# Expert outputs summed on chip instead of through a DRAM tensor, with another layout of the chunks

## The chip, the cores and the metric

The kernel runs on one core of one Trainium2 chip. The metric is the device time of one execution in microseconds (us); the kernel before has a median of 1822.23 us in 3 runs (1821.59 to 1824.75).

## The reference, cut to what matters

Two layers stand one behind the other: a hybrid layer (state-space part and attention), and a block of depth 2 whose second feed-forward part is a mixture of experts. Everything is float32. Only the mixture is touched by the change: 256 tokens, 8 experts, each token goes to its two best experts, and the two results are summed with softmax weights. Then follow a gated embedding term and a layer norm.

```python
logits = (xf @ w_router).astype(jnp.float32)
top_vals, top_idx = lax.top_k(logits, TOP_K)          # TOP_K = 2 of 8
gates = jax.nn.softmax(top_vals, axis=-1)
...
    def block_fn(args):
        tok, e = args
        xb = xf[tok]
        return (jax.nn.silu(xb @ w1[e]) * (xb @ w3[e])) @ w2[e]   # w1, w3: 1024 x 3584, w2: 3584 x 1024
...
y = y * gate_buf[:, None].astype(y.dtype)
out = jax.ops.segment_sum(y, tok_buf, num_segments=n)
...
e = jax.nn.sigmoid(h @ ple_gate_w[i] + ple_gate_b[i]) * (p[i] @ ple_w[i])
h = layer_norm(DEEPNORM_ALPHA * h + f + e, ln2_g[i], ln2_b[i])
```

## The kernel before

Weights come as chunks of 128 x 2048 float32 (1 MB). The dense layers take 135 of them (`N_DENSE`); each expert has 42 (`E_CHUNKS`): seven steps (`E_STEPS`) of four chunks for w1 and w3 (c = 0 to 3) and two for w2 (c = 4, 5). In the mixture stage the chunks lie in nine places (`LATE_RING`); the SP queue issues the load into a place once TensorE has used the chunk that lay there (`chunks_used`).

The router ranks the experts by how many tokens they got. Ranks 1, 2 (the two middle experts) and 0 (the fullest) are "heavy": 128 rows each, and rank 0 has 64 rows more. A heavy chunk is split in two rounded parts: ScalarE rounds it (line 2361), VectorE takes the rest (line 3273), three chunks ahead (`LOOK`), and TensorE makes three products of each block, 12 matmuls in all. Ranks 4, 3, 5, 6 are "small": 32 rows, or 64 for rank 3, straight float32, with the output divided into four or two tiles. What overflows, and the last rank, goes through a loop of lists of 64 rows (`MAX_TRIPS` at most, one trip with these inputs), whose loads and products follow the 294 static chunks.

The static order is laid out by `_merged_order` before anything runs: after each heavy chunk a counter rises by `HEAVY_LOAD` - `PACE` (30 - 24; for the fullest expert `BIG_LOAD` 49), and small chunks, each of which lowers it (by 24 - 20 or 24 - 12), are put in until it is at or below zero. `AT[kind, step, c]` is a chunk's number in the order. Work between the chunks is hung on these numbers: `GATHER_AT` (TensorE gathers the rows of a list with a 0/1 matrix from VectorE, line 1617, into banks 6 and 7), `PLACES_AT` (transposes for the last list's weights), `HEAVY_TURN_AT` and `TURN_AT` (transposes of the hidden tiles, lines 1725 and 1638), and `EMBED_AT` (six embedding operations of the pool engine, lines 736 to 744).

Each list's output goes from its PSUM banks into an SBUF tile (`ysb`, `y_big`, `y_small`, `y_64`), and the pool engine's queue stores it in the DRAM tensor `y_rows` (lines 785 to 797). `ysb` and `y_small` are used again, so the copy of a later list waits for the store of an earlier one. At the end of each loop trip four indirect DMAs gather, for both token tiles and both choices, the 1024-wide rows from `y_rows` (line 811), and VectorE adds them to `fe` with weights (line 3311). Only the last list's 64 rows are combined on chip: TensorE multiplies `selT` with `y_small` (line 1796), and `last_norm` adds banks 0 to 3 to `fe` and norms it.

In the loop, a trip starts when VectorE has chosen the rows (`x_sel`); then TensorE gathers them (16 matmuls), ScalarE copies them to `loop_x`, and the 42 chunks follow in `LOOP_ORDER`.

Of the kernel before, what the change touches and what calls it, by code (L numbers as in the profile page):

```python
# [25 lines left out]
P = 128  # L26
# [33 lines left out]
Y_ROWS = EXTRA_ROW + (MAX_TRIPS - 1) * HALF  # L60
ZEROED = 16 * ((Y_ROWS - SPARE_ROW) // P)
# [32 lines left out]
C_ALL = C_PAIR + 2 * H_ATT  # L94
# [74 lines left out]
GATHERS = ((ROW_QUARTERS, P), (0, P), (ROW_64, P), (2 * P, P))  # L169
GATHER_AT = (AHEAD - 1, 12, 20, AT["heavy", E_STEPS - 1, 1])  # L170
# [5 lines left out]
def _hi_slots():  # L176

    used, slots = [-1, -2, -3, -3], {}
    for m in HEAVY:
# [3 lines left out]
        else:  # L183
# [6 lines left out]
Y_DONE = sorted([(AT["heavy", E_STEPS * e + E_STEPS - 1, 5], "heavy", e) for e in range(3)]  # L190
                + [(AT["small", E_STEPS * l + E_STEPS - 1, 5], "small", l) for l in range(N_SMALL)])
Y_PARTS = [TILED[n] if kind == "small" else 3 if n == 2 else 1 for _, kind, n in Y_DONE]
Y_STORES = sum(Y_PARTS)


def stored_by(kind, n):

    k = [part[1:] for part in Y_DONE].index((kind, n))
    return ZEROED + 16 * sum(Y_PARTS[:k + 1])


# [64 lines left out]
def build(nc, x, meta, consts, vecs, srow, rows, bv, tbias, pT, w_dense, w_moe, out):  # L266
    with ExitStack() as ctx:
        y_rows = nc.dram_tensor("y_rows", (Y_ROWS, D), F32).ap()

# [131 lines left out]
        xgT, xgR = rounded("xgT", 4096, KT, P), rounded("xgR", 26624, KT, P)  # L401
# [56 lines left out]
        def many(ap, n, axis=-1):  # L458
# [13 lines left out]
        ld_x, ld_meta, ld_cst, ld_vec, ld_small, x_in, moe_dma = (sem(n) for n in (  # L472
            "ld_x", "ld_meta", "ld_cst", "ld_vec", "ld_small", "x_in", "moe_dma"))
# [18 lines left out]
            "sums_in squares w_hi w_lo places m_g m_xga m_xgv m_ya m_yv m_cb m_fe y_kept x_sel x_run"  # L492
# [152 lines left out]
        def _(pool):  # L645
# [135 lines left out]
            def keep_tiled(first, y, n):  # L781

                for c in range(n):
                    cs, rs_ = slice(D // n * c, D // n * (c + 1)), slice(P // n * c, P // n * (c + 1))
                    pool.dma_start(y_rows[bass.ds(first, P // n), cs], y[rs_, 0:D // n]).then_inc(moe_dma, 16)

            for _, kind, n in Y_DONE:
                if kind == "small":
                    wait(pool, "s_y", n + 1)
                    keep_tiled(FIRST_ROW[n], y_small, TILED[n])  # L790
                elif n < 2:
                    wait(pool, "m_ya", n + 1)
                    wait(pool, "m_yv", n + 1)
                    pool.dma_start(y_rows[(n + 1) * P:(n + 2) * P, :], ysb).then_inc(moe_dma, 16)
                else:
                    wait(pool, "b_y", 2)
                    pool.dma_start(y_rows[0:P, :], y_big).then_inc(moe_dma, 16)
# [21 lines left out]
        def _(pe):  # L819
# [848 lines left out]
            def heavy_first(m, u, c):  # L1668

                d = u - MID_STEPS  # L1670
                if c == 0:
# [7 lines left out]
                    elif d > 0:  # L1679
                        wait(pe, "b_hT64", d)  # L1680
# [1789 lines left out]
```

## Time and profile before

| | |
|---|---|
| median of 3 runs | 1822.23 us |
| the profiled execution | 1822.1 us, its span 1820.3 us |
| TensorE (PE) busy | 1723.2 us, 95% |
| VectorE (DVE), ScalarE (ACT) | 986.4 us, 54%; 774.7 us, 43% |
| moved by DMA | 522.14 MB, 287 GB/s over the span |
| HBM read, written | 511.20 MB, 5.37 MB |
| chain that ended last | PE 70%, DMA 17%, DVE 6%, ACT 4% |

Times in the profile are microseconds from the span's start. PE is TensorE, PEld its weight loads, POOL the pool engine, SP the engine whose queue issues the weights. A busy share of matmuls is not the array's peak. DMA queue q1 is that of the weights, q0 the pool engine's (software) queue, q8 fetches instructions. The mixture stage is what happens after 940 us.

### The profile page before, as it was taken

The numbers are of one execution on the slowest core, as the hardware profiler recorded it, in microseconds if no ns is written. First come the engines' busy times: TensorE is split into PE (matmuls) and PEld (weight loads), VectorE is DVE, ScalarE is ACT, GpSimd is POOL, SyncE is SP. The second block draws the span as 40 slices with busy tenths as digits, with TensorE's granted clock in tenths as the row PEclk, the third lists the DMA queues.
The fourth block names the chain that finished last, engine by engine and source line by source line (L and its number), as shares of the span: only waits on it lengthen the run. The fifth ranks groups of instructions, "written<-read, shape, count | busy, mean of one in ns | idle before, by whom it ended". The sixth has DMA issues, their size and how long they took to land.

```text
span 1820.3 us, 30869 instructions
## 1 busy us (share of the span) xinstructions
PE 1723.2 (95%) x13024; PEld 1335.3 (73%) x13024; DVE 986.4 (54%) x1173; ACT 774.7 (43%) x995; POOL 148.6 (8%) x130
## 2 busy tenths in 40 slices
PE   9999999999999999999999999998989989998876
PEld 8977888777888899989878777776645656665532
DVE  6867643467767655577676676775222333332103
ACT  7766533345346433344735465653222232332001
POOL 0033000000102410000200000112000000000100
PEclk9999999999999999999999999999999999999899
DMA  6532474423672655558249999999999999999996
GB/s 255 197 116 93 162 251 177 166 90 122 242 236 91 239 185 185 185 180 279 78 160 407 411 421 416 419 421 421 420 421 420 421 420 420 420 419 414 411 421 258
DMA packets 78282, 522.14 MB, mean 287 GB/s; under 512 B 9264, under 2 KB 12592, under 8 KB 17600
## 3 DMA queue, kind: packets, MB, share of 16 engines
q1 hardware_dynamic: 72128, 499.50, 69.4%
q0 software_dynamic: 5408, 19.60, 3.0%
q8 instruction: 103, 1.69, 0.4%
q10 hardware_dynamic: 608, 1.07, 0.2%
q14 instruction: 35, 0.29, 0.0%
HBM read 511.20 MB, written 5.37 MB: 284 GB/s over the span
## 4 chain that ended last, share of the span: by engine, by line
PE 70%; DMA 17%; DVE 6%; ACT 4%; issue 3%; POOL 0%; DVEq 0%; ACTq 0%; SPq 0%
PE bank L836 62%; DMA arena<-in_w_moe 8%; DMA ring<-in_w_moe 8%; ACT whi L2361 2%; PE bank L1617 1%; PE bank L1051 1%; DVE wrest L2418 1%; DVE whi L3273 1%; PE bank L1415 1%; DVE wrest L3273 1%; DMA cst<-in_consts 1%; PE bank L1725 0%; PE bank L1054 0%; PE bank L1139 0%; PE bank L1638 0%
## 5 line engine op out<-in xcount | busy, mean ns | idle before, releaser
L2361 ACT ACTIVATE whi<-ring 128x2048 fp32r<-128x2048 f32 x82 | 156.6, 1914 | 176.9 <-DMA ring<-in_w_moe 176.9
L836 PE MATMUL bank<-ring,arena 128*32 128x128 f32 (+2 forms) x2600 | 181.4, 324 | 12.6 <-DMA ring<-in_w_moe 11.4
L3273 DVE TENSOR_TENSOR wrest<-ring,whi 128x2048 fp32r<-128x2048 f32 x54 | 127.4, 2361 | 81.5 <-ACT whi L2361 81.5
L836 PEld LDWEIGHTS bank<-ring,arena 128*32 128x32 f32 (+1 forms) x2600 | 110.9, 121 | 82.3 <-issue 41.1
L836 PE MATMUL bank<-hTh,wrest 128*128 128x256 f32 x608 | 169.7, 279 | 0.0
L3273 DVE TENSOR_TENSOR whi<-ring,whi 128x2048 fp32r<-128x2048 f32 x28 | 64.2, 2293 | 126.4 <-ACT whi L2361 126.4
L2418 DVE TENSOR_TENSOR wrest<-ring,fhi 128x2048 fp32r<-128x2048 f32 x33 | 76.9, 2331 | 80.9 <-ACT fhi L1831 80.8
L836 PEld LDWEIGHTS bank<-hTh,wrest 128*128 128x128 f32 x608 | 115.4, 190 | 0.0
L836 PE MATMUL bank<-whi,xgT 128*128 128x512 f32 x280 | 105.7, 410 | 3.1 <-issue 2.1
L836 PE MATMUL bank<-hTh,fhi 128*128 128x256 f32 x352 | 99.1, 281 | 0.0
L836 PE MATMUL bank<-hTr,fhi 128*128 128x256 f32 x352 | 98.8, 281 | 0.0
L1831 ACT ACTIVATE fhi<-ring 128x2048 fp32r<-128x2048 f32 x33 | 63.1, 1915 | 77.5 <-PE bank L836 77.5
L836 PE MATMUL bank<-whi,big_x 128*128 128x512 f32 x336 | 86.8, 408 | 9.7 <-DVE whi L3273 9.7
L836 PE MATMUL bank<-whi,hidE 128*128 128x512 f32 x232 | 86.5, 418 | 7.8 <-DVE hidR L3222 6.1
L836 PE MATMUL bank<-uTh,wrest 128*128 128x272 f32 (+1 forms) x320 | 89.4, 287 | 0.0
L836 PE MATMUL bank<-whi,xgR 128*128 128x512 f32 x224 | 88.8, 396 | 0.0
L836 PEld LDWEIGHTS bank<-whi,big_x 128*128 128x128 f32 x336 | 61.9, 191 | 31.4 <-DVE whi L3273 9.4
L2418 DVE TENSOR_TENSOR wrest<-ring,lhi 128x2048 fp32r<-128x2048 f32 x20 | 45.9, 2293 | 71.3 <-ACT lhi L1839 71.3
L836 PE MATMUL bank<-wrest,uTh 128*128 128x512 f32 (+1 forms) x208 | 82.0, 394 | 0.0
L836 PE MATMUL bank<-arena 128*32 128x128 f32 (+3 forms) x1168 | 80.8, 306 | 1.2 <-DMA arena<-in_w_moe 1.0
L3273 DVE TENSOR_TENSOR whi<-arena,whi 128x2048 fp32r<-128x2048 f32 x23 | 54.6, 2372 | 47.0 <-ACT whi L2361 46.8
L1839 ACT ACTIVATE lhi<-ring 128x2048 fp32r<-128x2048 f32 x20 | 38.3, 1916 | 78.3 <-PE bank L836 78.3
(569 smaller groups left out, 4146.3 us busy)
## 6 DMA issues: line engine op xcount, KB each, us to landing
ring<-in_w_moe SPq DMA_DIRECT2D x224, 1024.0 KB, 13.0
ring<-in_w_dense SPq DMA_DIRECT2D x135, 1024.0 KB, 4.8
arena<-in_w_moe SPq DMA_DIRECT2D x75, 1024.0 KB, 13.1
row<-in_w_moe SPq DMA_DIRECT2D x37, 1024.0 KB
row<-in_rows POOLq DMA_DIRECT2D x17, 512.0 KB, 5.6
arena<-arena SPq DMA_DIRECT2D x32, 106.5 KB, 4.1
arena<-in_tbias POOLq DMA_DIRECT2D x2, 1536.0 KB, 8.9
y_rows<-ncR POOLq DMA_DIRECT2D x3, 512.0 KB, 13.5
```

What stands on the lines that cost most here:

```text
L836: ins = pe.matmul(out_, lhsT, rhs, start=start, stop=stop, **more)
L1051: ins = pe.matmul(ps[5][:, r * HD:(r + 1) * HD], dec[:, j, r * P:(r + 1) * P], xdt[:, j, r * HD:(r + 1) * HD], start=True, stop=True, skip ...
L1415: S["s_ps"].on(pe.matmul(score_bank(u), q2[:, hh, j * P:(j + 1) * P], k2[:, hh // 2, :], start=True, stop=True))
L1617: ins = pe.matmul(ps[bank][:, at_:at_ + width], h[:, j, k * P:(k + 1) * P], sel[:, j, 0:width], start=j == 0, stop=j == 1, skip_group_chec ...
L1831: S["w_hi"].on(a.activation(hi, ring[:, c % RING, :], ACT.Copy))
L1839: S["w_hi"].on(a.activation(l1_hi(c), ring[:, c % RING, :], ACT.Copy))
L2361: S["w_hi"].on(a.activation(late_hi(b), late_raw(b), ACT.Copy))
L2418: S["w_lo"].on(v.tensor_tensor(wrest[:, s, :], ring[:, s, :], hi.bitcast(F32), ALU.subtract))
L3273: S["w_lo"].on(v.tensor_tensor(late_rest(b), late_raw(b), late_hi(b).bitcast(F32), ALU.subtract))
```

## The change

`y_rows`, its stores, its zero filling and the indirect gathers go. Each list's output is added to `fe` by way of TensorE: a picking matrix `selT` (rows of the list x 256 tokens, with the token's weight where it chose that row) times the output tile gives 128 tokens x 512 columns in a bank, which VectorE adds to `fe`.

- At chunk 36 TensorE spreads each token's row number and weight over all partitions (8 matmuls with a broadcast operand instead of two transposes), and VectorE keeps them as `all_dest`, `all_gate`. A picking matrix is then three VectorE operations of 128 x 256 (`pick`), with the row numbers in `row_id` (three new columns of the constants).
- The middle experts are summed in four rounds (`MID_ROUNDS`, chunks 90, 94, 134, 138 of the new order), each of two matmuls over 128 rows into two banks, then two additions.
- The fullest expert, its 64 rows and three small lists are summed in banks 0 to 3 by five `join`s at chunks 272, 275, 278, 281, 284 (`JOIN_AT`), behind the fullest expert's end, the fourth small list by a sixth after the last static chunk; four additions take the banks to `fe`. Lists of 32 rows are multiplied in two groups with a wait between them (`quarter_pieces`).
- The small lists have tiles of their own (`y_lists`), the second middle expert its own pair of gathered rows (`mid_x`), rounded right behind its gather instead of after the first expert's last use of the pair.
- The loop's first list is gathered at chunk 288, the next trip's at (4, 3) of each trip; the list before the loop's current one is summed at (2, 3).
- `PACE` is 24.8 instead of 24, so the whole order changes, and `EMBED_AT` moves from 78 to 117 to 46 to 85.

```diff
-EMBED_AT = (78, 86, 94, 102, 110, 117)
+EMBED_AT = (46, 54, 62, 70, 78, 85)
 LISTED_AT, CHOSEN_AT, PLACES_AT = 24, 30, 36
-FIRST_LOAD, HEAVY_LOAD, BIG_LOAD, SMALL_LOAD, PACE = 36, 30, 49, {2: 20, 4: 12}, 24
+FIRST_LOAD, HEAVY_LOAD, BIG_LOAD, SMALL_LOAD, PACE = 36, 30, 49, {2: 20, 4: 12}, 24.8
...
+BIG_DONE = _last("heavy", 2)
+MID_ROUNDS = (EMBED_AT[-1] + 5, EMBED_AT[-1] + 9, _last("heavy", 1) + 4, _last("heavy", 1) + 8)
+JOIN_AT = tuple(BIG_DONE + 3 + 3 * n for n in range(5))
+PICK_AT = (EMBED_AT[-1] + 4, _last("heavy", 1) - 2) + tuple(m - 2 for m in JOIN_AT) + (JOIN_AT[-1] + 2,)
+N_SUMS = len(MID_ROUNDS) + len(JOIN_AT) + 1
+N_ADDS = len(MID_ROUNDS) + 1
+GATHERS = ((ROW_QUARTERS, P), (0, P), (ROW_64, P), (2 * P, P), (EXTRA_ROW, HALF))
+GATHER_AT = (AHEAD - 1, 12, 20, AT["heavy", E_STEPS - 1, 1], JOIN_AT[-1] + 4)
...
+        mid_x = ((rounded("xgT", 4096, KT, P), rounded("xgR", 26624, KT, P)),
+                 (rounded("next_xgT", 2048, KT, P), rounded("next_xgR", 3072, KT, P)))
...
-            with pool.Fori(0, trips) as t:
-                wait(pool, "s_y", t + (N_SMALL + 1))
-                keep_tiled(t * HALF + SPARE_ROW, y_small, 2)
-                pool.wait_ge(moe_dma, t * 32 + (ZEROED + 16 * (Y_STORES + 2)))
-                S["y_kept"].on(pool.nop())
-                for n in range(4):
-                    pool.indirect_dma_start(yg[n], None, y_rows, bass.IndirectOffsetOnAxis(from_i[:, n:n + 1], 0)) \
-                        .then_inc(tb_in, 16)
-                pool.wait_ge(tb_in, t * 64 + (32 + 64))
...
+            def quarter_pieces(picks, y, stop):
+
+                for n in range(2):
+                    for q in range(4):
+                        t, c = divmod(q, 2)
+                        rows_ = half_columns(2 * c + n, QUARTER)
+                        ins = pe.matmul(ps[q][:, half_columns(n, SEQ)], picks[rows_, t * P:(t + 1) * P], y[rows_, :],
+                                        start=False, stop=stop, skip_group_check=True)
+                    if n == 0:
+                        S["c_half"].on(ins)
+                        pe.wait_ge(S["c_half"].sem, S["c_half"].n)
+                return ins
+
+            def mid_round(k):
+
+                e, t = divmod(k, 2)
+                wait(pe, "c_sel", e + 1)
+                wait(pe, "m_ya", e + 1)
+                wait(pe, "m_yv", e + 1)
+                wait(pe, "c_add", k if t else 0)
+                for c in range(2):
+                    ins = pieces(ps[(6, 2)[e] + c], 1, selT[e], ysb, t, c, True, True)
...
+            def join(k):
+
+                wait(pe, "c_sel", k + 3)
+                picks = selT[k % 2]
+                if k == 0:
+                    wait(pe, "b_y", 2)
+                    for q in range(4):
+                        ins = pieces(ps[q], 1, picks, y_big, q // 2, q % 2, True, False)
+                else:
+                    pe.wait_ge(S["c_ps"].sem, S["c_ps"].n)
+                    if k == 1:
+                        wait(pe, "b_whole", 1)
+                    else:
+                        wait(pe, "s_y", k - 1)
+                    if k in (1, 3):
+                        for q in range(4):
+                            ins = pieces(ps[q], 2, picks, y_64 if k == 1 else y_lists[1], q // 2, q % 2, False, False)
+                    else:
+                        ins = quarter_pieces(picks, y_lists[k - 2], k == 5)
+                S["c_ps"].on(ins)
...
+                    if (j, c) == (2, 3):
+                        wait(pe, "c_sel", t + (len(PICK_AT) + 1))
+                        wait(pe, "c_add", t + N_ADDS)
+                        for q in range(4):
+                            ins = pieces(ps[q], 2, selT[0], y_small, q // 2, q % 2, True, True)
+                        S["c_ps"].on(ins)
+                    elif (j, c) == (4, 3):
+                        wait(pe, "x_sel", t + (len(GATHERS) + 1))
+                        gather_list(HALF)
...
+            def pick(n, id_at, step):
+
+                step(v.scalar_tensor_tensor(second_T, all_dest[1], row_id[:, id_at:id_at + 1], all_gate[1],
+                                            ALU.is_equal, ALU.mult))
+                step(v.scalar_tensor_tensor(selT[n], all_dest[0], row_id[:, id_at:id_at + 1], all_gate[0],
+                                            ALU.is_equal, ALU.mult))
+                return v.tensor_tensor(selT[n], selT[n], second_T, ALU.add)
+
+            def pick_static(number):
+
+                if number:
+                    v.wait_ge(S["c_sel"].sem, number)
+                else:
+                    wait(v, "ple_done", 20)
+                    wait(v, "places", 3)
+                if number > 3:
+                    wait(v, "c_ps", number + 1)
+                S["c_sel"].on(pick(number % 2, number, fin))
...
+            def add_rows(bank, t, c):
+
+                cs = slice(512 * c, 512 * c + 512)
+                return v.tensor_tensor(fe[:, t, cs], fe[:, t, cs], bank[:, :], ALU.add)
+
+            def add_round(k):
+
+                e, t = divmod(k, 2)
+                wait(v, "c_ps", k + 1)
+                wait(v, "c_add", k)
+                for c in range(2):
+                    ins = add_rows(ps[(6, 2)[e] + c], t, c)
+                S["c_add"].on(ins)
```

## Rows read from the trace of the kernel before

**Rows 1.** The page's GB/s, in 40 slices of 45.5 us.

```profile
GB/s 255 197 116 93 162 251 177 166 90 122 242 236 91 239 185 185 185 180 279 78 160 407 411 421 416 419 421 421 420 421 420 421 420 420 420 419 414 411 421 258
```

**Rows 2.** Windows: busy us of PE, PEld, DVE, ACT, POOL; clock, DMA share, GB/s.

```profile
1000.00:1180.00 180.00, 173.57 (x1370) 131.61 (x1371) 127.13 (x109) 99.75 (x77) 8.13 (x2) 0.99 1.01 417
1600.00:1700.00 100.00, 87.45 (x1023) 58.92 (x1022) 30.52 (x29) 24.56 (x27) 2.58 (x5) 0.97 1.01 413
1740.00:1780.00 40.00, 30.55 (x218) 15.03 (x218) 0.84 (x2) 1.54 (x4) 0.00 (x0) 1.00 1.01 420
```

**Rows 3.** TensorE's products of whi and xgT: count, ns, first and last start.

```profile
L836 PE MATMUL bank<-whi,xgT x280: 387/395/628, 957.1 to 1296.5; 128*128 128x512 f32 x140
```

**Rows 4.** Timeline at the end: start, us, what.

```profile
1804.44 1.94 PE L836 MATMUL bank<-arena,bvr 128*64 128x512 f32 x8 [0.45 <-DMA arena<-in_w_moe]
...
1807.25 1.99 PE L1796 MATMUL bank<-arena 64*128 64x512 f32 x8 [0.87 <-ACT arena L2374]
```

**Rows 5.** DMA queues, 900 to 1820 us: packets, MB, share.

```profile
q0 software_dynamic: 1680, 4.85, 1.3%
q8 instruction: 57, 0.93, 0.4%
```

**Rows 6.** DMA queues, 1700 to 1806 us.

```profile
q0 software_dynamic: 800, 2.49, 5.9%
```

**Rows 7.** Timeline, last static chunk to the loop's first product.

```profile
1691.98 0.43 DVE L3256 COPY arena<-bank 128x256 f32<-128x256 f32 x1 [3.25 <-PE bank L836]
...
1694.29 6.58 PE L1617 MATMUL bank<-arena,h 128*128 128x64 f32 x32 [2.38 <-DVE arena L3298]
...
1701.64 5.37 PE L836 MATMUL bank<-ring,arena 128*64 128x256 f32 x32 [0.77 <-ACT arena L2366]
```

**Rows 8.** Timeline of TensorE in the static list.

```profile
1198.34 1.08 PE L836 MATMUL bank<-ring,arena 128*32 128x128 f32 x32
1199.35 0.50 PE L836 MATMUL bank<-whi,hidE 128*128 128x512 f32 x1
...
1205.13 1.08 PE L836 MATMUL bank<-ring,arena 128*32 128x128 f32 x32
...
1234.90 1.95 PE L836 MATMUL bank<-arena 128*64 128x256 f32 x16
1236.68 1.90 PE L836 MATMUL bank<-ring,arena 128*64 128x256 f32 x16
...
1601.83 1.95 PE L836 MATMUL bank<-arena 128*64 128x256 f32 x16
1603.70 0.33 PE L1638 MATMUL bank<-cst,arena 128*128 128x128 f32 x1
```

**Rows 9.** Chain of work, a gather of 128 rows.

```profile
1104.67 3.57 PE bank L1617 x32
```

**Rows 10.** Waits of TensorE, 1060 to 1160, then 1160 to 1260: total, times.

```profile
PE bank L836 <- issue: 2.1, 1, 2.1
...
PE bank L1638 <- DVE arena L3203: 5.5, 1, 5.5
```

**Rows 11.** VectorE by form, 942 to 1700 us: busy us, mean ns.

```profile
L3273 DVE TENSOR_TENSOR whi<-ring,whi 128x2048 fp32r<-128x2048 f32 x28 | 64.2, 2293 | 126.4 <-ACT whi L2361 126.4
...
L3203 DVE TENSOR_TENSOR arena<-arena,bank 128x256 f32<-128x256 f32 x7 | 2.9, 417 | 10.4 <-ACT arena L2283 10.4
```

**Rows 12.** Timeline of VectorE beside the pool engine's embedding.

```profile
1158.41 4.50 DVE L3273 TENSOR_TENSOR wrest<-ring,whi 128x2048 fp32r<-128x2048 f32 x1
...
1213.21 3.86 DVE L3273 TENSOR_TENSOR wrest<-ring,whi 128x2048 fp32r<-128x2048 f32 x1
...
1250.21 4.15 DVE L3273 TENSOR_TENSOR whi<-arena,whi 128x2048 fp32r<-128x2048 f32 x1 [0.20 <-ACT whi L2361]
```

**Rows 13.** DMA issues, 1000 to 1100, then 1100 to 1200: us to landing.

```profile
ring<-in_w_moe SPq DMA_DIRECT2D x28, 1024.0 KB, 11.9
...
ring<-in_w_moe SPq DMA_DIRECT2D x27, 1024.0 KB, 11.0
```

More of the change, by code:

```diff
@@ L168, with _last @@
 HEAVY_TURN_AT = [AT["heavy", u + 1, 0] if u < MID_STEPS else AT["heavy", u, 3] + 2 for u in range(HEAVY_STEPS)]
-GATHERS = ((ROW_QUARTERS, P), (0, P), (ROW_64, P), (2 * P, P))
-GATHER_AT = (AHEAD - 1, 12, 20, AT["heavy", E_STEPS - 1, 1])
+def _last(kind, n):
+    return AT[kind, E_STEPS * n + E_STEPS - 1, 5]
+BIG_DONE = _last("heavy", 2)
[6 more added lines that the diff above has]
+GATHER_AT = (AHEAD - 1, 12, 20, AT["heavy", E_STEPS - 1, 1], JOIN_AT[-1] + 4)
+assert _last("heavy", 0) < MID_ROUNDS[0] and MID_ROUNDS[1] + 1 < AT["heavy", MID_STEPS, 0]
+assert MID_ROUNDS[3] < AT["heavy", MID_STEPS, 4] and GATHER_AT[-1] < STATIC and _last("small", 2) < JOIN_AT[2]
 EVICTED = (2, 4)
@@ L189 @@
 HI_SLOT = _hi_slots()
[L190 to L199, printed above, removed]
 LOOP_ORDER = [part for j in range(E_STEPS) for part in [(j, c) for c in range(4)] + ([(j - 1, 4), (j - 1, 5)] if j else [])]
@@ L778, in _ @@
                         power(rstd[:, j:j + 1], 1)
[L781 to L797, printed above, removed]
-                    wait(pool, "b_whole", 1)
-                    keep_tiled(ROW_64, y_64, 2)
-                pool.wait_ge(moe_dma, stored_by(kind, n))
-            wait(pool, "places", 2)
-            wait(pool, "router_done", 2)
-            trips = pool.value_load(plan_i[0:1, ID_TRIPS:ID_TRIPS + 1], min_val=1, max_val=MAX_TRIPS)
-            with pool.Fori(0, trips) as t:
-                wait(pool, "s_y", t + (N_SMALL + 1))
-                keep_tiled(t * HALF + SPARE_ROW, y_small, 2)
-                pool.wait_ge(moe_dma, t * 32 + (ZEROED + 16 * (Y_STORES + 2)))
-                S["y_kept"].on(pool.nop())
-                for n in range(4):
-                    pool.indirect_dma_start(yg[n], None, y_rows, bass.IndirectOffsetOnAxis(from_i[:, n:n + 1], 0)) \
-                        .then_inc(tb_in, 16)
-                pool.wait_ge(tb_in, t * 64 + (32 + 64))
             for j in range(2):
@@ L1752, in _ @@
                         wait(pe, "b_xv", 2)
+                    elif g == 3:
+                        wait(pe, "places", 3)
                     else:
-                        wait(pe, "places", 3)
+                        wait(pe, "b_hT64", E_STEPS)
                     gather_list(GATHERS[g][1])
@@ L2324, in keep_mid @@
                 finished("heavy", E_STEPS * e + E_STEPS - 1, 5)
-                if e:
-                    a.wait_ge(moe_dma, stored_by("heavy", 0))
+                wait(a, "c_ps", 2 * e)
                 S["m_ya"].on(a.activation(ysb[:, 0:512], ps[2][:, :], ACT.Copy))
@@ L3192, in combination @@
-                fin(ins)
-                S["places"].on(v.tensor_tensor(selg[:, :, :], selg[:, :, :], selT[:, :, :], ALU.add))
+                firsts = [(0, P), (0, 2 * P), (0, 0), (1, ROW_64)]
+                firsts += [(n // 2, first) for n, first in zip(TILED, FIRST_ROW)] + [(1, EXTRA_ROW - 2 * HALF)]
+                for n, (kind, first) in enumerate(firsts):
+                    ins = v.tensor_scalar(row_id[:, n:n + 1], cst[:, C_ROW + kind:C_ROW + kind + 1], float(first), None, ALU.add)
@@ L3369, in _constants @@
     c[:META, C_TOM + META:C_PAIR] = 1.0
+    for n, rows in enumerate((P, HALF, QUARTER)):
+        c[:, C_ROW + n] = t % rows
     for m in range(H_ATT):
```

153 lines of the change are left out of this document (79 added, 74 removed).

## The prediction

> **What bounds the kernel now.** I read the speed of the transfers first. From slice 22 of 40 on, the core moves about 420 GB/s without a break [rows 1]; by windows the 16 DMA engines are busy all the time while TensorE's share falls from 97% to 76% [rows 2]. This is the expert stage: 336 weight chunks of 1024 KB, 1.0486 MB / 420.5 GB/s = 2.494 us each. The reader is to see two things at once. The transfers set the end, but only because TensorE keeps up: at 1000 to 1180 it is busy 173.6 of 180 us. So I then read what TensorE does per chunk, which waits it has, and how far the landings are ahead of it.
>
> The span is 1820.3 us and the profiled execution 1822.1, the median of the runs 1822.23; sums are made against the span, and 1.8 us are added. TensorE starts the stage at 957.1 [rows 3], ends it at 1804.44 + 1.94 = 1806.4, and 13.9 us of closing work follow [rows 4]. That closing work is copied unchanged (its picking matrix is ready long before), so it stays 13.9.
>
> **What goes: traffic.** All stores to y_rows and the four indirect gathers are software DMAs; the stage's q0 has 4.85 MB [rows 5]. At 420 GB/s that is 11.5 us of a saturated stream. The last stretch alone has 2.49 MB in 5.9% of 106 us, 6.3 us against 5.9 by bytes [rows 6], so bytes are a fair price; between 11 and 12.5 us. The zero fills of y_rows ran hundreds of us earlier, under TensorE work: nothing. The hand-over from the static list to the loop goes too: TensorE's last static product ends near 1692, the vector engine chooses rows, the gather takes 6.58 us at half clock, and the first loop product starts at 1701.64 [rows 7]. Meanwhile the window 1600 to 1700 moves 413 instead of 420 GB/s [rows 2], 1.7 us lost; after the change the loop's list is gathered at chunk 288. Gain at most 11.5 + 1.7 = 13.2.
>
> **What comes: TensorE work.** The layout number 24.8 instead of 24 puts fewer light (small-list) chunks between heavy ones. Counting the order as the program lays it out: the fullest expert ends at chunk 269 instead of 286, the middle two at 66 and 130 instead of 70 and 153. Durations [rows 8]: a light chunk of four tiles 1.01 us; two heavy ones behind it 5.78, which I split as 2.77 each, 0.19 for a heavy chunk behind a light one, 0.05 left over; a two-tile chunk 1.78, in longer series 1.74; the fullest expert's 64-row part adds 1.8. Up to chunk 269 the new order holds 84 x 2.77 + 42 x (2.77 + 1.82) + 81 changes x 0.19 + 102 x 1.02 + 42 x 1.74 = 618.0; turns of hidden tiles 24 x 0.33 [rows 8] and 21 of about 0.5 = 18.4; four gathers of rows at 3.57 = 14.3. Together 650.7. The old order had 630.2 in the same 270 chunks. New operations: a gather is 16 f32 matmuls of 128 columns in 3.57 us [rows 9], 0.22 each, so one of 512 columns is 0.9. Four mid rounds have eight: 7.2. At chunk 36 eight 128-column broadcasts stand for two transposes: 1.8. Sum 659.7 us, 2.44 per chunk against 2.494 of a landing: there is 13 us of room where there was 42.
>
> **Stalls.** From 1000 to 1180 TensorE idles 6.4 us of 180, 3.6% [rows 2], and between 1160 and 1260 one wait alone, for a gated tile, is 5.5 [rows 10]; an idle stretch is followed by a stretch at 1.2 GHz, each costing 1 to 2 us more. One stall goes: 2.1 us before the second middle expert, waiting for rounded rows that now have their own pair of buffers and are rounded at chunk 56 [rows 10]. I take 29 us (4.4%), between 20 and 38.
>
> **What hides the rest.** Joins: behind chunk 269 stand 24 light chunks, of 1.05 us against 2.494, room for 34 us. Five joins cost 3.6 (128 rows) and 4 x 2.0 (the closing product, four 64-row matmuls, takes 1.99 [rows 4]; for the 32-row ones the bounds are 1.9 and 3.6), and the loop's gather up to 3.7: 15, hidden. Without that cover all 15 would show. In the loop, TensorE is busy 30.55 of 40 us [rows 2], 0.59 us free per chunk; the four pieces (2.0) have 24 chunks behind them and the loop's gather, now at (4, 3) and useless in the only trip, has 14 (8 us) for at most 3.7. The vector engine gets ten picks (eight in the static list) of three 128x256 operations (0.42 each [rows 11], so 1.3 to 1.6), sixteen additions of 128x512 at about 0.7 and loses the copies' waits. Ahead of its weight splitting a pick can delay a heavy chunk; it is 71% busy between 1000 and 1180 [rows 2], and I put this into the stalls. POOL's stores go, and with them every wait of the vector engine and ScalarE for a store. POOL's six embedding operations move from chunks 78 to 117 to 46 to 85. In the trace three vector splittings beside such POOL work take 4.50, 3.86 and 4.15 us [rows 12] where the usual one takes 2.29 [rows 11].
>
> The Trainium skill (SBUF — State Buffer, SBUF: two separate sides) says that a vector operation with two SBUF inputs and a GpSimd operation exclude each other for the whole instruction; the trace agrees in kind, with at most 2.2 us extra and three of six POOL operations hit. By the rule all six could block, about 20 us of vector time at rows' durations, in the tighter place.
>
> The Trainium skill (TensorEngine Tiling (Array Packing), Key Properties) says that changing the tiling mode drains TensorE. The trace shows 0.19 us for light to heavy; with that for each join and each return the sum would rise by about 2 us, all under cover.
>
> **The sum.** TensorE ends chunk 269 at 957.1 + 659.7 + 29 = 1645.8. Nine places hold chunks, 9 x 2.494 = 22.4 us of supply; a landing takes 11.0 to 11.9 us after its issue when TensorE is slow to free places [rows 13], so the load is some 11.4 ahead: chunk 269 landed at 1634.4. 66 more landings at 2.494 are 164.6, instruction fetch 0.4% of it [rows 5] 0.7: 1799.7. The last chunk's product 2.0: 1801.7, against 1806.4 before: 4.7 us less. 1822.1 - 4.7 = 1817.4.
>
> **Rivals.** (B) All of it is gained: the stalls are mostly waits for DMA in disguise and TensorE keeps the pace; then 1822.1 - 13.2 = 1808.9. For it: 2.44 us of work per chunk leave room. Against it: 2.44 us plus 3.6% is 2.53, over 2.494. (C) No change: TensorE loses what the transfers gave, stalls of 34 us instead of 29, or the middle experts' end drags on; 1822. For it: the landings' margin. (D) Slower: in the middle stage, chunks 20 to 150, TensorE becomes the bound, the vector engine's splitting falls behind beside POOL and the picks, each miss costs 2 us idle and 1 to 2 at half clock. From 9 us of stalls above my 29 on, it is slower than 1825.9; at 12 above it is 1829. Against it: the 34 us of room of the light tail lets the loads run again, but a lost load slot is not won back. (E, counted with D) The stores and gathers were free, since reads and writes have their own room: then only TensorE's added work counts, 29 us at most and its last 8 us at least, and the end is case D's; the flat 420 GB/s in total with and without q0 [rows 1, 6] speaks against.
>
> **How the numbers follow.** The forecast's case 0.45 (1812 to 1821), B 0.15, C 0.21, D with E 0.19. A measurement of this kernel can tell 0.2%, 3.6 us, from no change. Of the forecast's case 0.38 lies under 1818.6, with B's 0.15 and 0.01 of C: faster 0.54; same 0.27; slower 0.19. The range goes from 1809.5, just over the full gain, to 1827, which takes in the mild part of D.
>
> **What would show it.** Right: the stage's transfers fall by 4.85 MB and no indirect DMA is left; DMA share under 1.00 or GB/s under 415 somewhere in 1000 to 1350; TensorE busy 96% or more there; the fullest expert's last product at 1640 to 1650; the first loop product without a pause behind the last static one; the tail 13.9 us. Wrong: 420 GB/s everywhere (then B), the big expert's end after 1655 (D), or idle of more than 3 us at joins or at (2, 3) of the loop.

## The result, and the profile after

The changed kernel takes 1808.47 us (median of 6 runs, 1807.59 to 1808.68), the kernel before 1822.03 beside it (6 runs, 1821.06 to 1824.87): a ratio of 0.9922, 95% interval 0.9911 to 0.9932. That is 13.6 us less, where 4.7 were predicted, and 1.0 us under the low end of the range. It is almost to the microsecond the time of rival B, 1808.9. The profiled execution has a span of 1806.7 us and a time of 1808.6.

The page's GB/s in 40 slices of 45.2 us; the row of before is [rows 1]:

```profile
GB/s 257 196 119 94 163 233 163 163 96 123 205 266 71 250 187 187 188 163 270 131 102 408 418 420 412 421 421 420 421 413 421 420 421 420 420 420 420 421 420 256
```

Windows of the changed kernel, columns as in [rows 2] (busy us of PE, PEld, DVE, ACT, POOL; clock, DMA share, GB/s):

```profile
1000.00:1180.00 180.00, 177.93 (x1322) 137.91 (x1321) 139.16 (x114) 104.33 (x80) 16.94 (x6) 1.00 1.01 418
1600.00:1700.00 100.00, 88.14 (x1115) 56.42 (x1115) 27.70 (x48) 12.56 (x19) 0.00 (x0) 0.90 1.01 420
```

From 1000 to 1180 TensorE is busy 177.9 us of 180, 4.4 more than before [rows 2], and the transfers are not slower for it (418 GB/s, 417 before). From 1600 to 1700 the dent is gone: 420 GB/s instead of 413.

DMA queues of the changed kernel, 900 to 1810 us; the software queue q0 with its 4.85 MB [rows 5] has no line any more:

```profile
q1 hardware_dynamic: 49104, 355.49, 94.4%
```

Timelines of the changed kernel: the fullest expert's last product; the hand-over from the static list to the loop (before: [rows 7]); the end (before: [rows 4]):

```profile
1634.33 1.94 PE L800 MATMUL bank<-row,arena 128*64 128x512 f32 x8
...
1686.68 1.59 PE L800 MATMUL bank<-ring,bvr 128*32 128x256 f32 x16 [2.64 <-DMA ring<-in_w_moe]
...
1688.89 4.21 PE L1712 MATMUL bank<-arena 32*128 32x256 f32 x16 [0.62 <-DVE arena L3305]
...
1693.03 4.48 PE L800 MATMUL bank<-ring,arena 128*64 128x256 f32 x20
...
1790.97 1.94 PE L800 MATMUL bank<-arena,bvr 128*64 128x512 f32 x8 [0.45 <-DMA arena<-in_w_moe]
...
1793.68 1.99 PE L1703 MATMUL bank<-arena 64*128 64x512 f32 x8 [0.78 <-ACT arena L2403]
```

The reader is to see: chunk 269 is done at 1636.3, not at 1645.8; behind the last static chunk TensorE goes from the last join straight into the loop; the last expert product ends at 1792.9 (before 1806.4), and 13.8 us of closing work follow (before 13.9).

### The profile page after: what moved, and what is told of

Read it like the earlier page. It is cut to its first block, busy times and chain, and to the rows that moved or that the text cites. A ratio compares the mean times of both kernels' runs of the same rounds, so it can differ in the third digit from the quotient of the medians.

```text
span 1806.7 us, 31172 instructions
## 1 busy us (share of the span) xinstructions
PE 1742.4 (96%) x13166; PEld 1350.7 (75%) x13166; DVE 1004.4 (56%) x1222; ACT 774.0 (43%) x995; POOL 128.3 (7%) x102
## 4 chain that ended last, share of the span: by engine, by line
PE 79%; DMA 9%; DVE 6%; ACT 3%; issue 2%; POOL 0%; DVEq 0%; SPq 0%; ACTq 0%
PE bank L800 69%; DMA ring<-in_w_moe 5%; DMA arena<-in_w_moe 4%; ACT whi L2390 1%; DVE wrest L3322 1%; DVE whi L3322 1%; PE bank L1581 1%; PE bank L1015 1%; PE bank L1703 1%; DVE wrest L2447 1%; PE bank L1379 1%; PE bank L903 0%; PE bank L1018 0%; PE bank L1602 0%; PE bank L1692 0%
## 5 line engine op out<-in xcount | busy, mean ns | idle before, releaser
L800 PE MATMUL bank<-ring,arena 128*32 128x128 f32 (+2 forms) x2984 | 193.6, 319 | 6.8 <-DMA ring<-in_w_moe 6.3
L2390 ACT ACTIVATE whi<-ring 128x2048 fp32r<-128x2048 f32 x80 | 151.9, 1915 | 71.2 <-DMA ring<-in_w_moe 66.1
L800 PEld LDWEIGHTS bank<-ring,arena 128*32 128x32 f32 (+1 forms) x2984 | 121.9, 120 | 80.4 <-issue 42.0
L3322 DVE TENSOR_TENSOR whi<-ring,whi 128x2048 fp32r<-128x2048 f32 x25 | 57.3, 2293 | 86.6 <-ACT whi L2390 86.6
L800 PE MATMUL bank<-whi,hidE 128*128 128x512 f32 x264 | 91.4, 405 | 8.3 <-DVE hidR L3275 8.3
L3322 DVE TENSOR_TENSOR whi<-arena,whi 128x2048 fp32r<-128x2048 f32 x27 | 61.8, 2290 | 66.0 <-ACT whi L2390 66.0
L2314 ACT ACTIVATE arena<-bank 128x128 f32<-128x128 f32 (+1 forms) x35 | 11.2, 319 | 185.0 <-PE bank L800 185.0
L3256 DVE TENSOR_TENSOR arena<-arena,bank 128x128 f32<-128x128 f32 (+1 forms) x35 | 11.9, 339 | 139.8 <-ACT arena L2314 139.8
L800 PEld LDWEIGHTS bank<-whi,big_x 128*128 128x128 f32 x336 | 61.9, 191 | 24.2 <-issue 10.4
L654 POOL TENSOR_TENSOR rstd<-rstd,neg_half 128x1 f32<-128x1 f32 x10 | 16.1, 1617 | 837.8 <-DVE rstd L2419 837.8
## 6 DMA issues: line engine op xcount, KB each, us to landing
ring<-in_w_moe SPq DMA_DIRECT2D x224, 1024.0 KB, 11.8
```

What stands on the lines that cost most here:

```text
L654: S["pow_done"].on(pool.tensor_tensor(ap, ap, neg_half[:, 0:1].to_broadcast([P, n]), ALU.pow))
L800: ins = pe.matmul(out_, lhsT, rhs, start=start, stop=stop, **more)
L2390: S["w_hi"].on(a.activation(late_hi(b), late_raw(b), ACT.Copy))
L3256: S["s_hid"].on(v.tensor_tensor(hid_small[:, 0:512 // n], sl_small[:, 0:512 // n], ps[4][:, 512 // n:1024 // n], ALU.mult))
L3322: S["w_lo"].on(v.tensor_tensor(late_rest(b), late_raw(b), late_hi(b).bitcast(F32), ALU.subtract))
```

## The experiments

Times are medians; the ratio is to the kernel before in the same comparison, whose medians there were 1821.5, 1822.5 and 1821.8 us. The last column is against the kernel named, by medians. Since the kernel before drifted by 1 us between the comparisons, the ratios give the rows against the changed kernel somewhat differently: +12.4, +11.7, +12.0, +39.0, +1.6, 0.0, +14.0, +0.7, +0.7, +12.6. Differences of 1 us are not told apart by this table.

| kernel | us | ratio and interval | difference |
|---|---|---|---|
| 4.98 MB of stores added early | 1820.02 | 0.9990 (0.9981 to 0.9998) | changed +11.6 |
| the same added late | 1819.55 | 0.9986 (0.9978 to 0.9995) | changed +11.1 |
| before, layout 24.8 alone | 1822.54 | 1.0003 (0.9995 to 1.0012) | before +1.0 |
| before, its bytes gone | 1811.84 | 0.9943 (0.9931 to 0.9956) | before -9.7 |
| mid rounds three times | 1821.30 | 0.9988 (0.9979 to 0.9998) | changed +12.8 |
| mid rounds seven times | 1848.83 | 1.0136 (1.0121 to 1.0152) | changed +40.4 |
| loop's gather at its head | 1811.14 | 0.9931 (0.9917 to 0.9945) | changed +2.7 |
| one pair of buffers | 1809.67 | 0.9922 (0.9909 to 0.9936) | changed +1.2 |
| 16 products spread | 1821.59 | 0.9999 (0.9990 to 1.0008) | changed +13.1 |
| mid rounds on 16 columns | 1808.56 | 0.9926 (0.9913 to 0.9939) | changed +0.1 |
| changed, layout 24.4 | 1808.51 | 0.9926 (0.9913 to 0.9938) | changed 0.0 |
| changed, layout 25.2 | 1820.71 | 0.9991 (0.9983 to 1.0000) | changed +12.2 |

### What a byte costs: stores added to the changed kernel

```diff
+            for n, m in enumerate([12, 19, 26, ... 138]):
+                pool.wait_ge(chunks_used.sem, N_DENSE + m)
+                pool.dma_start(more[n * P:(n + 1) * P, :], cst[:, 0:512]).then_inc(more_out, 16)
```

> The changed kernel with 19 added stores of a constant 128x512 tile (0.262 MB each, 4.98 MB in all) to a DRAM tensor of its own, issued by POOL at chunks 12, 19, ... 138 of the expert stage; nobody waits for them but POOL at its end. Theory A, the stage is bound by its bytes from the first chunk to the last: 4.98 MB / 420.5 GB/s = 11.8 us, so 1808.5 + 11.8 = 1820.3 us. Rival B, TensorE sets the pace of chunks 0 to 150 (its busy share is 98% there and the transfers run at 416 to 418 GB/s): bytes added there are hidden in part, and no more than 6 us show, 1811 to 1814.5.

The second kernel has the same stores at chunks 296, 298, ... 332.

> The changed kernel with the same 19 added stores (4.98 MB), now issued at chunks 296, 298, ... 332, in the loop, where TensorE is idle for a fifth of the time. Both theories (bytes bound the whole stage; TensorE bounds its first 150 chunks) give 11.8 us more, 1820.3 us. A third, that writes to DRAM have room of their own beside the reads, gives 1808.5 to 1811 us here and in the kernel with the early stores, and then the gain of the change came from something else than its removed traffic.

DMA queues of the kernel with early stores, 900 to 1820 us:

```profile
q0 software_dynamic: 1520, 4.98, 1.3%
```

Early they cost 11.6 us, late 11.1, against 11.8 by bytes: 2.3 us for a MB, wherever it moves. Theory A holds; neither do writes have room of their own, nor does TensorE hide bytes in the first 150 chunks. The prediction's price of the traffic, 11.5 us for 4.85 MB, is confirmed.

### The kernel before with one part each

```diff
-FIRST_LOAD, HEAVY_LOAD, BIG_LOAD, SMALL_LOAD, PACE = 36, 30, 49, {2: 20, 4: 12}, 24
+FIRST_LOAD, HEAVY_LOAD, BIG_LOAD, SMALL_LOAD, PACE = 36, 30, 49, {2: 20, 4: 12}, 24.8
```

> The kernel before with the layout number 24.8 instead of 24 and nothing else. Theory A (bytes bound the stage): the added TensorE work of the first 270 chunks is covered by landings, no change, 1820 to 1823 us. Rival B (TensorE bounds the middle): slower, by the 22 us of heavy work that move ahead of chunk 130 less the idle time of TensorE, 3 to 10 us, 1825 to 1832. Rival C (the new order itself took TensorE's stalls away, 39 us of waits before, 20 after): faster by 2 us or more, under 1820.

```diff
-        y_rows = nc.dram_tensor("y_rows", (Y_ROWS, D), F32).ap()
+        y_rows = nc.dram_tensor("y_rows", (Y_ROWS, 16), F32).ap()
...
-                    pool.indirect_dma_start(yg[n], None, y_rows, bass.IndirectOffsetOnAxis(from_i[:, n:n + 1], 0)) \
+                    pool.indirect_dma_start(yg[n][:, 0:16], None, y_rows, bass.IndirectOffsetOnAxis(from_i[:, n:n + 1], 0)) \
```

> The kernel before, old layout and all its waits and issues, but each store and each of the four indirect gathers moves 16 columns of a row instead of up to 1024, so that the 4.85 MB of the stage are nearly gone (the last four sums take h in place of the fetched rows). Theory A: 4.85 MB less is 11.5 us, 1822.0 - 11.5 = 1810.5 us; the hand-over's 1.7 us stay. Rival B: only the bytes from the fullest expert's end on count, 2.5 MB or 5.9 us: 1816. Rival C (a good part of the 13.6 us came with the layout or the removed waits for stores): 1815 or more.

The layout alone does nothing to the time (rivals B and C of that run fall), the bytes alone bring 9.7 us by the medians, 10.4 by the ratio, whose interval (8.0 to 12.6) holds the 11.5 too. If it does fall short, its trace has a place for it: it moves 415 GB/s from 957 to 1340, where the kernel before and the changed one both move 417, which is 383 x 2 / 420.5 = 1.8 us.

But the layout did something to TensorE's waits. Waits of TensorE from 957 to 1640 us (total, times, longest), before:

```profile
PE bank L1638 <- DVE arena L3203: 16.2, 6, 5.5
PE bank L836 <- DVE whi L3273: 8.8, 12, 2.2
PE bank L836 <- DVE hidR L3222: 5.9, 5, 2.0
PE bank L1725 <- DVE arena L3211: 4.0, 4, 1.4
PE bank L836 <- DVE wrest L3273: 2.6, 4, 1.6
PE bank L836 <- issue: 2.1, 1, 2.1
```

The same view of the changed kernel:

```profile
PE bank L1602 <- DVE arena L3256: 8.9, 7, 3.3
PE bank L800 <- DVE hidR L3275: 8.3, 6, 1.7
PE bank L800 <- DVE whi L3322: 2.2, 2, 1.6
PE bank L800 <- DVE wrest L3322: 0.4, 1, 0.4
```

39.6 us before, 19.8 after. The kernel before with the new layout has 26.2, without its bytes 34.1: 13.4 and 5.5 us less, together 18.9 of the 19.8. Each total is that of one traced execution. With the layout alone TensorE is busy 656.7 us from 957 to 1640, 643.3 before: 13.4 us more work is done by then, 13.4 us of waits are gone, and the time is the same. What was being waited for shows one engine further. ScalarE's largest wait in the same stretch, before:

```profile
ACT whi L2361 <- DMA ring<-in_w_moe: 161.5, 56, 16.0
```

The same wait in the changed kernel:

```profile
ACT whi L2390 <- DMA ring<-in_w_moe: 66.1, 31, 9.5
```

With its two other lines for landings ScalarE's splitting waits 209 us for landings before, 145 with the layout alone, 189 with the bytes gone, 128 after. Here is how such a wait reaches TensorE; timeline of the kernel before around one of its two longest pauses:

```profile
1359.15 1.89 PE L836 MATMUL bank<-row,bvr 128*64 128x512 f32 x8
1361.83 1.91 ACT L2361 ACTIVATE whi<-ring 128x2048 fp32r<-128x2048 f32 x1 [16.04 <-DMA ring<-in_w_moe]
1363.65 0.37 ACT L2283 ACTIVATE arena<-bank 128x256 f32<-128x256 f32 x1
1363.78 2.29 DVE L3273 TENSOR_TENSOR whi<-ring,whi 128x2048 fp32r<-128x2048 f32 x1 [15.82 <-ACT whi L2361]
1365.98 0.41 DVE L3203 TENSOR_TENSOR arena<-arena,bank 128x256 f32<-128x256 f32 x1
1366.45 0.69 PE L1638 MATMUL bank<-cst,arena 128*128 128x128 f32 x2 [5.42 <-DVE arena L3203]
```

TensorE's 5.4 us are booked on the gated tile (L3203). The gated tile stands behind a splitting of the vector engine, its SiLU behind one of ScalarE, and that one had waited 16 us for a landing. TensorE stopped at 1361.0 and the chunk landed at 1361.8: 0.8 us of the pause are the landing itself, the other 4.6 are the two splittings, the SiLU and the gating that stood in order behind it. The pause was set off by a transfer. The other long one, in front of 1254.7 [rows 10], is of mixed kind: the splittings of ScalarE ahead of it waited 3.6 and 0.6 us for landings, both before TensorE stopped at 1249.3, and the vector engine's splitting at 1250.21 [rows 12] took 1.9 us more than the usual 2.29. The changed kernel has no pause over 1.8 us before chunk 269 but one of 3.3.

### How much room TensorE has

```diff
                 for c in range(2):
-                    ins = pieces(ps[(6, 2)[e] + c], 1, selT[e], ysb, t, c, True, True)
+                    for _ in range(3):
+                        ins = pieces(ps[(6, 2)[e] + c], 1, selT[e], ysb, t, c, True, True)
```

> The changed kernel with the eight products of the four mid rounds (chunks 90, 94, 134, 138) issued three times each: 16 more matmuls of 128x512, 0.95 us each by the rounds' rows (1.9 for two), 15.2 us of TensorE work more in the middle of the stage, same result. Theory A (there is room: 2.44 us of work a chunk against 2.494 of a landing): the added work is covered by the lead of the loads, 1808.5 to 1811 us. Rival D (the middle is at its edge, each late chunk frees its place late and a lost load slot is not won back): 15.2 less what the vector engine catches up in it (some 3 to 6 us) shows, 1817 to 1821 us.

The next kernel has range(7).

> The changed kernel with the products of the four mid rounds issued seven times each: 45.6 us of TensorE work more at chunks 90 to 138. Theory A: beyond the room of about 13 us (by the prediction's sum) plus the 20 us of TensorE's waits the rest shows, 1808.5 + 13 to 33 = 1821 to 1841 us. Rival D: nearly all of it shows, 1808.5 + 40 to 45 = 1848 to 1854 us. Together with the kernel of three rounds it gives the price of one us of TensorE work there.

The added work is less than was reckoned there. A round of the kernel with tripled rounds, from its first product to the next chunk's, then one of the changed kernel:

```profile
1184.35 5.31 PE L1703 MATMUL bank<-arena 128*128 128x512 f32 x12
1189.10 0.80 PE L800 MATMUL bank<-whi,hidE 128*128 128x512 f32 x1
```

```profile
1185.03 1.88 PE L1703 MATMUL bank<-arena 128*128 128x512 f32 x4
1186.35 0.80 PE L800 MATMUL bank<-whi,hidE 128*128 128x512 f32 x1
```

4.75 us against 1.32 are 3.43 more a round (0.86 for a product, which the profile lists as two), 13.7 us for the four, not 15.2; with seven times 41.2, not 45.6 (1184.65 to 1196.27 is 11.62 us).

Windows of the kernel with tripled rounds:

```profile
1180.00:1260.00 80.00, 79.49 (x542) 58.01 (x541) 55.86 (x37) 42.84 (x33) 0.00 (x0) 1.00 0.96 392
1260.00:1340.00 80.00, 78.82 (x501) 46.56 (x501) 25.31 (x24) 17.60 (x20) 0.00 (x0) 1.00 0.94 380
```

Theory A (room) falls, rival D (the edge) stands: 12.8 of 13.7 us show, 40.4 of 41.2. Between the two kernels 27.5 us of work cost 27.5: each us costs one us. Carried back at that price, the added work begins to cost at 13.7 - 12.8 = 0.9 us; by the ratios it is 1.7, and with their intervals (0.1% either way, 1.8 us) the room is known to about 2 us. The loss sits where the work is: 392 and 380 GB/s where the changed kernel has 420 and 416. TensorE's waits did not shrink much under the load either: 16.4 us and 15.8, against 19.8. What went is one pause: the changed kernel's longest, 3.3 us in front of 1415.96, behind a splitting of ScalarE that had waited 9.5 us for a landing. Some 16 us, booked on turned, gated and rounded tiles, stay whatever is added at these chunks; whether work elsewhere would fill them was not tried.

```diff
+MORE_AT = tuple(range(70, 87, 2)) + tuple(range(98, 117, 3))
...
+                if m in MORE_AT:
+                    wait(pe, "c_add", 2 if m > MID_ROUNDS[1] else 0)
+                    pe.matmul(ps[6][:, :], h[:, 0, 0:P], h[:, 0, 0:512], start=True, stop=True, skip_group_check=True)
```

> The changed kernel with 16 added matmuls of 128x512 in an unused bank, 0.95 us each, 15.2 us in all, issued one by one at chunks 70 to 86 (every second) and 98 to 116 (every third): the same work as in the kernel with tripled rounds (which took 12.8 us more), but spread instead of in four bursts of 3.8 us. If the mean load of TensorE in the middle is at its edge, it costs the same 11 to 13 us: 1819.5 to 1821.5. If only bursts hurt and there is room on average, as the prediction's 2.44 against 2.494 us a chunk says, 2 to 6 us: 1810.5 to 1814.5.

Spread out, 16 products of 0.86 us, 13.8 in all, cost 13.1 us (14.0 by the ratio): no matter of bursts. Window of this kernel, then of the changed one:

```profile
957.00:1340.00 383.00, 379.36 (x2744) 278.49 (x2742) 247.02 (x219) 191.54 (x153) 17.23 (x6) 1.00 1.00 404
```

```profile
957.00:1340.00 383.00, 378.39 (x2799) 279.22 (x2799) 250.65 (x219) 194.65 (x155) 16.94 (x6) 1.00 1.01 417
```

383 x 13 / 420.5 = 11.8 us of load slots lost, and not won back. TensorE's busy share is the same 99% in both, so it doesn't tell on which side of the edge a kernel is; the GB/s does.

```diff
-                    ins = pieces(ps[(6, 2)[e] + c], 1, selT[e], ysb, t, c, True, True)
+                    ins = pe.matmul(ps[(6, 2)[e] + c][:, 0:16], selT[e][:, t * P:(t + 1) * P], ysb[:, 512 * c:512 * c + 16],
+                                    start=True, stop=True, skip_group_check=True)
```

> The changed kernel with the eight products of the mid rounds on 16 columns instead of 512, so that the sums of the two middle experts are left out but for 16 columns: TensorE has 7 us less to do at chunks 90 to 138, everything else stays. If one us of TensorE work there is worth 0.84 us on this side too (as between single, tripled and sevenfold rounds), 1808.5 - 6 = 1802.5 us. If there is a knee, since the transfers already run at 416 to 418 of 420.5 GB/s between 957 and 1340, only what they lack can come back: 0 to 3 us, 1805.5 to 1808.5.

```diff
-FIRST_LOAD, HEAVY_LOAD, BIG_LOAD, SMALL_LOAD, PACE = 36, 30, 49, {2: 20, 4: 12}, 24.8
+FIRST_LOAD, HEAVY_LOAD, BIG_LOAD, SMALL_LOAD, PACE = 36, 30, 49, {2: 20, 4: 12}, 24.4
...
-JOIN_AT = tuple(BIG_DONE + 3 + 3 * n for n in range(5))
+JOIN_AT = tuple(BIG_DONE + 3 + 2 * n for n in range(5))
```

> The changed kernel with the layout number 24.4 instead of 24.8: the second middle expert ends at chunk 140 instead of 130, the fullest at 277 instead of 269, some 14 us of TensorE work less in the first 270 chunks; the joins follow at every second chunk instead of every third and the loop's gather at chunk 292. If the stage is bound by bytes but for the 1% that TensorE takes in the middle: 0 to 3 us less, 1805.5 to 1808.5. If the shorter light tail (16 chunks instead of 24 behind the fullest expert) can't take the joins: 1810 or more, with a pause in front of the loop.

The third has the number 25.2 and nothing else.

> The changed kernel with the layout number 25.2: the fullest expert ends at chunk 261 instead of 269, some 14 us of TensorE work more in the first 262 chunks, taken from the light tail. If TensorE's waits there are elastic (waits for weights that had not landed, which more work fills): 1808.5 to 1811. If the whole stretch to the fullest expert's end is at its edge like chunks 90 to 138: 0.84 of it shows in part, 1814 to 1820.

Less TensorE work brings nothing, by 7 us or by the layout: there is a knee, and bytes alone set the time below it. The 7 us that are missing turn up as waits. TensorE's two largest from 957 to 1640 in the kernel with short rounds:

```profile
PE bank L1602 <- DVE arena L3257: 11.7, 7, 3.1
PE bank L800 <- DVE hidR L3276: 10.0, 6, 2.6
```

All its waits are 25.3 us, 5.5 more than the changed kernel's 19.8, and its last product of chunk 269 ends at 1637.8, not before the changed kernel's 1636.3. Heavy work packed more closely costs 12.2 us, a little more than the dearer of the two cases on record, 1814 to 1820; the other (elastic waits would take 14 us more) missed. It had taken the room for the whole stretch; it is lost at one place. Windows of the kernel with 25.2, then its timeline:

```profile
1260.00:1280.00 20.00, 16.85 (x149) 11.97 (x138) 9.36 (x9) 6.74 (x8) 0.00 (x0) 0.83 0.96 378
1280.00:1300.00 20.00, 19.92 (x147) 12.08 (x140) 5.15 (x6) 4.12 (x4) 0.00 (x0) 1.00 0.91 349
1300.00:1320.00 20.00, 17.29 (x112) 10.47 (x114) 6.58 (x7) 3.05 (x4) 0.00 (x0) 1.00 0.85 328
```

```profile
1266.22 1.90 ACT L2390 ACTIVATE whi<-ring 128x2048 fp32r<-128x2048 f32 x1
...
1268.16 2.29 DVE L3322 TENSOR_TENSOR wrest<-ring,whi 128x2048 fp32r<-128x2048 f32 x1 [4.46 <-ACT whi L2390]
...
1270.70 0.48 PE L1602 MATMUL bank<-cst,arena 128*128 128x128 f32 x1 [3.15 <-DVE arena L3256]
...
1275.67 0.63 PE L800 MATMUL bank<-whi,hidR 128*128 128x512 f32 x1
1276.10 0.60 PE L800 MATMUL bank<-whi,hidE 128*128 128x512 f32 x1
...
1278.16 0.39 PE L800 MATMUL bank<-whi,hidR 128*128 128x512 f32 x1
1278.38 0.39 PE L800 MATMUL bank<-whi,hidE 128*128 128x512 f32 x1
```

A pause of 3.2 us behind two queued splittings (no landing in it this time), then the lower of TensorE's two clocks, 1.2 GHz: starts of 512-column products 0.43 us apart instead of 0.23, for 13 of them, 2.6 us more. That is case D as the prediction describes it, 5.8 of the 12.2 us. A second pause, 2.2 us in front of 1302.1, makes it 8.0. From 1260 to 1340 this kernel moves 360 GB/s where the changed one moves 416: 80 x 56 / 420.5 = 10.7 us of load slots, nearly the whole loss. Between the pauses TensorE has no gap to speak of (19.92 of 20 us) and the transfers are still at 349 GB/s; how the rest divides between the pauses and the denser work I did not separate.

### The hand-over and the second pair

```diff
             with pe.Fori(0, trips) as t:
+                wait(pe, "x_sel", t + (len(GATHERS) + 1))
+                gather_list(HALF)
...
-                    elif (j, c) == (4, 3):
-                        wait(pe, "x_sel", t + (len(GATHERS) + 1))
-                        gather_list(HALF)
```

> The changed kernel with the loop's rows gathered at the head of the loop, as before: rows chosen by the vector engine after the last static product, gather of 32 small matmuls (3.8 us at full clock, up to 6.6 at half), rounding by ScalarE, then the loop's first product; the gather at (4, 3) of the loop goes. Theory A: TensorE pauses 8 to 13 us there as before (the first loop product starts that much after the last static one), the loads stop for 1 to 2 us because their places come free late: 1808.5 + 1.7 = 1810.2 us. Rival: the ring's nine places cover it entirely, 1808.5, or the pause brings a half-clock stretch and costs 3 us or more.

Timeline and window of that kernel at the hand-over; the changed kernel has 421 GB/s in the same window:

```profile
1696.17 7.09 PE L1581 MATMUL bank<-arena,h 128*128 128x64 f32 x32 [3.69 <-DVE arena L3360]
...
1704.02 4.28 PE L800 MATMUL bank<-ring,arena 128*64 128x256 f32 x24 [0.76 <-ACT arena L2393]
```

```profile
1690.00:1730.00 40.00, 33.91 (x232) 22.41 (x232) 6.17 (x16) 2.13 (x5) 0.00 (x0) 0.79 0.89 363
```

It costs 2.7 us by the medians, 1.6 by the ratios (its five runs lie between 1808.8 and 1813.3): the prediction's 1.7 or somewhat more. The profiled one, 1812.5 us, shows the rival's half-clock stretch: the gather takes 7.09 us where the changed kernel's takes 3.79, at a granted clock of 0.79 in the window.

```diff
-        mid_x = ((rounded("xgT", 4096, KT, P), rounded("xgR", 26624, KT, P)),
-                 (rounded("next_xgT", 2048, KT, P), rounded("next_xgR", 3072, KT, P)))
+        mid_x = 2 * ((rounded("xgT", 4096, KT, P), rounded("xgR", 26624, KT, P)),
+                 )
...
-                if m == GATHER_AT[3] + 1:
+                if m == AT["heavy", E_STEPS - 1, 3] + 1:
```

> The changed kernel with one pair of buffers for the rounded rows of both middle experts: the second expert's rows are rounded only after chunk (6, 3) of the first, as before. Theory A: TensorE waits some 2 us there, which the loads' lead covers, or costs at most 2 us of load slots, 1808.5 to 1810.5 us. Rival C' (this pair is what took the stalls of the middle away, 39 us of TensorE's waits before against 20 after, and what lifted the transfers from 413 to 417 GB/s between 957 and 1180): 1811 us or more, TensorE's waits up to chunk 269 at 25 us or more, and the transfers back at 413 to 415 GB/s there.

1.2 us by the medians, nothing by the ratio: no difference that can be told from none. Its TensorE waits are 18.1 us, so the pair is not what took the waits away.

## Why the prediction was wrong, point by point

**What bounds the kernel: right.** Bytes from chunk 0 to 335. The two kernels with stores and the one without bytes show it from both sides.

**Traffic 11.5, hand-over 1.7: right in size.** 11.1 to 11.6 us for 4.98 MB; 1.6 to 2.7. The parts measured one by one are 9.7 + 2.7 + 1.2 = 13.6 by the medians, 10.4 + 1.6 + 0.0 = 12.0 by the ratios, of a change of 13.6 or 14.2: they add up to within some 2 us, and the exact match of the medians is luck.

**TensorE's added work: right.** 659.7 us up to chunk 269 were counted; from 956.3 to 1636.3 are 680.0 us, less 19.8 of waits 660.2. Timeline of the changed kernel, two quarter joins and the loop's gather:

```profile
1651.21 2.33 PE L1712 MATMUL bank<-arena 32*128 32x256 f32 x16
...
1665.01 4.22 PE L1712 MATMUL bank<-arena 32*128 32x256 f32 x16
1674.85 3.79 PE L1581 MATMUL bank<-arena,h 128*128 128x64 f32 x32
```

A mid round is 1.88 [1185.03 above] against 1.8 (7.2 for four), the gather 3.79 against 3.7. A quarter join takes 2.3 us at full clock, 4.2 at half, over my bound of 3.6; it is hidden all the same.

**The stalls: this step failed.** "I take 29 us (4.4%), between 20 and 38": it carried the share of idle time of the old trace over to the new order and added it to the work, as if a stall belonged to the chunks. 19.8 came (what half clock costs is in the 660.2 of work). With transfers as the bound, half of before's waits were what TensorE had left over, and more work per chunk takes their place. The layout alone shows it: 13.4 us more work done by 1640, 13.4 less of waits, the same time. The short rounds show it from the other side: 7 us less work, 5.5 more of waits, the same time. The bytes gone take 5.5 us of waits away; by which way was not separated. Of the two long pauses one was set off by a landing, the other in part. With 20 instead of 29 the prediction's own sum gives 1645.8 - 9.2 = 1636.6 for the end of chunk 269 (measured 1636.3) and 1808.2 in all; that is no second proof, since the stage also began 0.8 us earlier than 957.1. Up to 1340 the half-clock stretches went with the pauses (granted clock 1.00 from 957 to 1340, 0.99 before); from 1600 to 1700, where the light chunks cover it, the clock is lower than before, 0.90 against 0.97 [rows 2]. The failed step could have been seen: ScalarE's 161.5 us of waits for landings and the 16 us in front of 1361.83 stand in the trace of before. I had read TensorE's waits and stopped at the engine they name.

**The room: reckoned without the waits.** "13 us of room where there was 42" (by its own numbers 13.7 and 43.2) compares work with landings. With work added in the middle 16 to 19 us of waits stay (16.4 and 15.8 in the rounds, 19.2 spread), and so the room measured is 1 us, within about 2.

**Rival B: right in number, and its reason right in half.** "The stalls are mostly waits for DMA in disguise" holds for about half of them, the 19.8 us that went. The argument against it, 2.44 + 3.6% = 2.53 over 2.494, was the failed step again.

**Rival D: the mechanism and its price are right, the distance to it was not.** It begins about 1 us of TensorE work above what the changed kernel has, at 1 us for each. For the prediction's point, 38 us of stalls, that gives 1808.5 + 17 = 1825.5, where its sum gives 1826.4. The change landed at 20, on the knee's good side, and that it stopped so near the edge without crossing it is luck.

**What I named as signs:** q0's 4.85 MB gone, the loop's product without a pause, the tail of 13.8 us and TensorE over 96% came. So did GB/s under 415 somewhere in 1000 to 1350: the page's row has 412 in its 25th slice (1084 to 1129) and 413 in its 30th (1310 to 1355). With them, 420 everywhere, the sign of B, did not come, though B's time did. The end of chunk 269 at 1640 to 1650 did not come.

**POOL's embedding: hidden, as taken.** Vector splittings beside it in the changed kernel:

```profile
1115.70 4.46 DVE L3322 TENSOR_TENSOR wrest<-ring,whi 128x2048 fp32r<-128x2048 f32 x1
...
1171.98 4.20 DVE L3322 TENSOR_TENSOR wrest<-ring,whi 128x2048 fp32r<-128x2048 f32 x1 [0.19 <-ACT whi L2390]
```

The Trainium skill (SBUF — State Buffer, SBUF: two separate sides) has such pairs exclude each other for a whole instruction; the trace agrees, at most 2.2 us each, and between 1100 and 1180 TensorE has no pause (80.00 of 80 us busy). Whether the later embedding of the kernel before cost anything was not tried by itself.

## What to carry to other kernels

Follow a stall back until an engine waits for a transfer or for nothing: if it ends at a transfer, more work can fill it and it is no term to add; if it ends at another engine's work, expect it to stay. Then look whether a kernel with a few us less work gets them back as waits. Where two limits lie within a per cent, measure the knee from both sides, by a few us of added work and a few taken away: here the change used up the room down to about 1 us, and the next 13.7 us of TensorE work in the middle cost 12.8. Lost load slots show as GB/s of a window, not in the busy share of either side.

## What the runs showed of the hardware

The DMA share says little near the edge: 1.00 at 404 GB/s (the spread work), 0.94 at 380, 1.01 at 420. So a byte took some 2 to 3% more engine time there; why is not shown.

With the layout number 25.2 TensorE fell to 1.2 GHz after a pause of 3.2 us, having been busy 79.0 of 80 us from 1180 to 1260, and lost 2.6 us more by it. The Trainium skill (TensorE: Matmul & The Clock Gate, HAM oscillation — how this bites in real kernels) has idle gaps bring the clock down; the trace agrees, and here it was a single gap.

The prediction has a stretch at 1.2 GHz behind an idle stretch as a rule; the length of the pause alone does not decide it. Timeline of the kernel before, two pauses of the same length in front of the same kind of products:

```profile
1460.05 3.07 PE L836 MATMUL bank<-whi,big_x 128*128 128x512 f32 x12 [2.18 <-DVE whi L3273]
...
1553.47 4.30 PE L836 MATMUL bank<-whi,big_x 128*128 128x512 f32 x12 [2.18 <-DVE whi L3273]
```

The granted clock is 1.00 from 1460 to 1470 and 0.83 from 1553 to 1563. What makes the difference is not shown.

The core drew 420 to 421 GB/s in 14 of the 18 full slices of the stage. The Trainium skill (Perfetto Trace Analysis, Roofline) puts the bound of a core's 16 DMA engines at about 435 GB/s in all when one core alone is active; by the traces it is 3% less for loads of 1 MB.
